# Memory attention of the decode rows: queries and probabilities as 32-column weights in four column groups

## The reference

```python
def _mem_attend(q, mk, mv):
    logits = jnp.einsum('bqhd,bshd->bhqs', q, mk.astype(q.dtype), preferred_element_type=jnp.float32) * (C_HD ** -0.5)
    p = jax.nn.softmax(logits, axis=-1)
    o = jnp.einsum('bhqs,bshd->bqhd', p.astype(q.dtype), mv.astype(q.dtype))
    return o.reshape(q.shape[0], q.shape[1], C_HEADS * C_HD)
...
    oc = _mem_attend(qc.reshape(Bsz, L, C_HEADS, C_HD), mem_k, mem_v)
```

## Time and profile before

| | us |
|---|---|
| median of 3 runs | 2118.42 |
| lowest, highest | 2112.59, 2127.39 |
| profiled execution, own time | 2127.54 |
| span of its profile | 2125.7 |
| mean granted clock of TensorE | 0.988 |
| decode stage in the profile, from the first gate product | 894.9 to 1078.9 |

### The profile page before, as it was taken

The page is one execution under the profiler, slowest core; times in us unless marked ns, Lnnn a source line. Parts: engine busy times, 40 slices in busy tenths (PEclk is TensorE's granted clock), DMA queues, the critical chain, the costliest instruction groups (busy, mean ns, idle before and its releaser), DMA issues.

```text
span 2125.7 us, 34336 instructions
## 1 busy us (share of the span) xinstructions
PE 2082.0 (98%) x13455; PEld 2011.8 (95%) x13455; DVE 999.6 (47%) x1765; ACT 524.6 (25%) x1143; POOL 737.0 (35%) x318
## 2 busy tenths in 40 slices
PE   6999999999999999999999999999999999999998
PEld 6999999999999999999889987999999999999997
DVE  5754720455555555411337945452534344343435
ACT  5333521344333344321032222200000000000002
POOL 3334763111111111121035432334444434444344
PEclk9999999999999999999799999999999999999999
DMA  6224333433222232263185431211111111111114
GB/s 194 79 80 111 105 97 110 128 101 102 73 64 85 83 102 66 60 172 118 60 273 192 161 138 62 72 41 49 39 49 39 49 47 46 45 49 39 49 40 174
DMA packets 221287, 193.79 MB, mean 91 GB/s; under 512 B 24731, under 2 KB 192283, under 8 KB 221170
## 3 DMA queue, kind: packets, MB, share of 16 engines
q1 hardware_dynamic: 207058, 182.72, 27.9%
q10 hardware_dynamic: 14128, 9.65, 1.4%
HBM read 146.26 MB, written 47.09 MB: 91 GB/s over the span
## 4 chain that ended last, share of the span: by engine, by line
PE 87%; DVE 6%; DMA 2%; issue 1%; ACT 1%; SPq 1%; POOL 0%; DVEq 0%; POOLq 0%; ACTq 0%
PE psum L1485 24%; PE psum L984 13%; PE psum L1546 11%; PE psum L1173 6%; PE psum L1101 6%; PE psum L1500 5%; PE psum L1251 4%; PE psum L1477 4%; PE psum L1220 2%; PE psum L1193 1%; PE psum L1209 1%; ACT pr L1817 1%; PE psum L1008 1%; PE psum L1049 1%; DVE asm L2282 1%
## 5 line engine op out<-in xcount | busy, mean ns | idle before, releaser
L842 POOL TENSOR_TENSOR wsp<-raw,kc 128x1024 fp32r<-128x1024 f32 x115 | 276.4, 2404 | 1151.8 <-PE psum L1173 423.5
L1485 PE MATMUL psum<-actD,wsp 128*128 128x352 f32 x3168 | 515.8, 323 | 1.0 <-ACT sg L2021 0.6
L1485 PEld LDWEIGHTS psum<-actD,wsp 128*128 128x128 f32 x3168 | 509.1, 188 | 1.5 <-issue 0.9
L845 POOL TENSOR_TENSOR wsp<-raw,wsp 128x1024 fp32r<-128x1024 f32 x115 | 281.8, 2451 | 9.0
L984 PE MATMUL psum<-actT,wsp 128*128 128x352 f32 x1656 | 272.7, 325 | 0.0
L984 PEld LDWEIGHTS psum<-actT,wsp 128*128 128x128 f32 x1656 | 267.9, 190 | 0.3
L2594 DVE TENSOR_TENSOR accT<-accT,psum 128x352 f32<-128x352 f32 x504 | 241.7, 520 | 50.1 <-PE psum L1546 50.1
L1546 PE MATMUL psum<-fT,wsp 128*128 128x352 f32 x1512 | 249.8, 323 | 0.4 <-DVE accT L2594 0.4
L1546 PEld LDWEIGHTS psum<-fT,wsp 128*128 128x128 f32 x1512 | 244.0, 188 | 0.7 <-DVE accT L2594 0.7
L1173 PE MATMUL psum<-actT,wsp 128*128 128x352 f32 x1152 | 216.5, 333 | 0.0
L2577 DVE TENSOR_TENSOR fr<-psum,sg 128x352 f32<-128x352 f32 x66 | 34.5, 524 | 375.4 <-PE psum L1485 373.1
(11 more groups left out here) (433 smaller groups left out, 2621.4 us busy)
## 6 DMA issues: line engine op xcount, KB each, us to landing
raw<-in_w_in SPq DMA_DIRECT2D x100, 256.0 KB, 4.0
raw<-in_w_ffn_in SPq DMA_DIRECT2D x88, 256.0 KB, 3.1
gat<-s_gate SPq DMA_DIRECT2D x12, 1056.0 KB, 5.1
raw<-in_w_ffn_out SPq DMA_DIRECT2D x44, 256.0 KB, 2.7
s_gate<-gst SPq DMA_DIRECT2D x48, 176.0 KB, 1.9
s_qkv<-y SPq DMA_DIRECT2D x12, 528.0 KB, 3.0
brw<-s_br SPq DMA_DIRECT2D x3, 2112.0 KB, 9.7
raw<-in_w_branch SPq DMA_DIRECT2D x24, 256.0 KB, 5.4
```

Of the source, the lines that this page charges most:

```text
L842: pool.tensor_tensor(wsp[:, slot, 0], raw[:, slot], ones.unsqueeze(1).to_broadcast([P, KT, P]), ALU.mult).then_inc(w_hi, 1)
L845: pool.tensor_tensor(wsp[:, slot, 1], raw[:, slot], wsp[:, slot, 0].bitcast(F32), ALU.subtract).then_inc(w_lo, 1)
L1485: mm = pe.matmul(psum[:, bank, 0:CH], wsp[:, slot, a, k, :], actD[:, h, k, CH * c:CH * c + CH], start=(k == 0 and q == 0), stop=(k == KT - ...
```

## The change

The scores turn the roles round: the queries become the weights and the transposed keys are streamed. `qw` holds for each head 8 blocks of 36 columns, zero but for the 4 query columns at the start of each. The 32 columns from 32 b on then hold the 4 queries of memory b in columns 4 b to 4 b + 3 and zeros elsewhere. The product for head h writes partitions 32 h to 32 h + 31 of bank 6 (one of four column groups), with all 256 keys streamed, and adds to what the other memories wrote there. So the rows of the softmax stand in bank 6 at once, and `mem_s`, the score transposes and the tile `mS` go. The values do the same with the probabilities: `pw`, one tile for each half of the memory, is filled by ACT from `mem_pt`, and the products stream 128 value columns of each head. Their sum has decode rows on partitions, so DVE copies it out (`mem_c`, tile `mC`) and one transpose (`mem_o`) follows. DVE fills `qw` and the second `pw` with zeros (`qw0`, `pw0`) and copies the queries (`qw`). The second `pw` shares `kvw` with the window keys, whose tile `wkv` is split for this.

The order changes too: the window scores alternate between rows 0 to 63 and 64 to 127 for each sequence, without the 14 gate products between; 20 gate products follow at once; `mem_values(6)` comes right behind `update(6)`, and `mem_values(7)` 14 gate products later and ahead of `update(7)`.

```diff
-    wkv = sb("wkv", [P, 2, DB, P], on=cE)
+    kvw = sb("kvw", [P, DB * P + 4 * DB * 36], on=cE)
+    kw_v, kw_k = (kvw[:, DB * P * x:DB * P * x + DB * P].rearrange("p (b d) -> p b d", b=DB) for x in range(2))
...
-    mS = sb("mS", [P, 2, P], on=cE)
...
-    pad = sb("pad", [P, 216], on=mid)
+    pad = sb("pad", [P, 344], on=mid)
...
+    mC = sb("mC", [P, P], on=mid)
+    qw = sb("qw", [P, 4, DB * 36], on=mid)
+    pw = (qw, kvw[:, DB * P:].rearrange("p (h x) -> p h x", h=4))
...
+    own_step = lambda ap: ap.rearrange("p h (b x) -> p h b x", x=36)[:, :, :, 0:DS]
...
             for h in range(4):
-                for t in range(2):
-                    mm = pe.matmul(psum[:, 5, P * t + DS * h + 16 * b:P * t + DS * h + 16 * b + DS], ckT[:, h, P * t:P * t + P],
-                                   da[:, 4 + h, DS * b:DS * b + DS], start=True, stop=True)
-            mm.then_inc(m_sc, 1)
+                mm = pe.matmul(psum[NS * h:NS * h + NS, 6, 0:MEM], qw[:, h, NS * b:NS * b + NS], ckT[:, h, :],
+                               start=(b == 0), stop=(b == DB - 1))
+            if b < DB - 1:
+                mm.then_inc(m_sc, 1)
+            else:
+                done(mm, "mem_rows")
...
-            for h in range(4):
-                for t in range(2):
-                    mm = pe.matmul(psum[:, 6, 2 * P + NS * h + DS * b:2 * P + NS * h + DS * b + DS], ck[:, b % 2, t, P * h:P * h + P],
-                                   mS[:, t, 16 * b + DS * h:16 * b + DS * h + DS], start=(t == 0), stop=(t == 1))
+            for t in range(2):
+                for h in range(4):
+                    mm = pe.matmul(psum[NS * h:NS * h + NS, 6, 2 * P:3 * P], pw[t][:, h, NS * b:NS * b + NS], ck[:, b % 2, t, P * h:P * h + P],
+                                   start=(b == 0 and t == 0), stop=(b == DB - 1 and t == 1))
...
-        for v in range(2):
-            rows = slice(64 * v, 64 * v + 64)
-            bank = (4, 7)[v]
-            for b in range(DB):
-                pe.matmul(psum[:, bank, 0:P].rearrange("p (g b s) -> p g b s", g=4, b=DB)[:, :, b, :], wkT[rows, b, :],
+        for b in range(DB):
+            for v, rows in enumerate((HA, HB)):
+                pe.matmul(psum[:, 4 + 3 * v, 0:P].rearrange("p (g b s) -> p g b s", g=4, b=DB)[:, :, b, :], wkT[rows, b, :],
                           da[rows, 0:4, DS * b:DS * b + DS], start=True, stop=True)
-            mm = pe.matmul(psum[0:Dn, bank, 256:256 + P], ext[rows, 0, :], da[rows, 0:4, :], start=True, stop=True)
-            if v == 0:
-                gate_mm(14)
+        for v, rows in enumerate((HA, HB)):
+            mm = pe.matmul(psum[0:Dn, 4 + 3 * v, 256:256 + P], ext[rows, 0, :], da[rows, 0:4, :], start=True, stop=True)
         done(mm, "new_sc")
-        gate_mm(6)
-        pe.wait_ge(f_ac, ACn("mem_s"))
-        for t in range(2):
-            mm = pe.transpose(psum[:, 6, P * t:P * t + P], mS[:, t, :], ident)
-        done(mm, "mem_rows")
-        gate_mm(14)
+        gate_mm(20)
...
         update(6)
-        gate_mm(6)
         mem_values(6)
+        gate_mm(14)
+        done(mem_values(7), "mem_v")
         gate_mm(10)
         update(7)
-        done(mem_values(7), "mem_o")
+        pe.wait_ge(f_dv, DVn("mem_c"))
+        done(pe.transpose(psum[:, 6, 3 * P:4 * P], mC[:], ident), "mem_o")
         gate_mm(576 - Gates.n)
...
-        act.wait_ge(m_sc, 1 + DB)
-        fdone(act.activation(flat(mS[:]), psum[:, 5, 0:256], ACT.Copy), "mem_s")
...
-        copy_e("mem_p", flat(mS[:]), psum[:, 6, 0:256], "mem_pt")
+        act.wait_ge(f_pe, PEn("mem_pt"))
+        act.wait_ge(f_dv, DVn("pw0"))
+        for t in range(2):
+            mm = act.activation(own_step(pw[t]), psum[:, 6, P * t:P * t + P].rearrange("p (h b s) -> p h b s", h=4, b=DB), ACT.Copy)
+        fdone(mm, "mem_p")
...
+        f("qw0", dve.memset(qw[:], 0.0))
+        own("qw0")
+        f("qw", dve.tensor_copy(own_step(qw), da[:, 4:8, :].rearrange("p h (b s) -> p h b s", b=DB)))
...
+        f("pw0", dve.memset(kvw[:, DB * P:], 0.0))
...
+            if j == 6:
+                dve.wait_ge(f_pe, PEn("mem_v"))
+                f("mem_c", dve.tensor_copy(mC[:], psum[:, 6, 2 * P:3 * P]))
...
-        f("mem_o", dve.tensor_copy(dob[:, 2], q4(6, 2, P)))
+        f("mem_o", dve.tensor_copy(dob[:, 2], q4(6, 3, P)))
```

More of the change, by code:

```diff
@@ L286, in build @@
     QI = (0, 1, 2, 3, 5, 6)
+    HA, HB = slice(0, 64), slice(64, 128)
     A_SC = [AHD ** -0.5] * 4 + [P ** -0.5] * 2
@@ L348, in build @@
     LOAD_G = {0: 18, 1: 19, 2: 20, 5: 21, 9: 22, 10: 23}
-    PE_E = ("out", "win_kt0", "bcast", "win_kt1", "x0", "new_sc", "mem_rows", "y", "win_rows", "xt", "mem_pt", "u_w",
-            "win_pt", "w_q_s", "vn", "win_o", "o", "sumsq", "mem_o")
-    AC_E = ("kv_out", "new_out", "tail_out", "wkT0", "dec", "rq", "wkT1", "mem_s", "x0", "win_s", "y", "mem_exp",
+    PE_E = ("out", "win_kt0", "bcast", "win_kt1", "mem_rows", "x0", "new_sc", "y", "win_rows", "xt", "mem_pt", "u_w",
+            "win_pt", "w_q_s", "vn", "win_o", "o", "sumsq", "mem_v", "mem_o")
+    AC_E = ("kv_out", "new_out", "tail_out", "wkT0", "dec", "rq", "wkT1", "x0", "win_s", "y", "mem_exp",
             "win_exp", "win_sk", "mem_p", "win_p", "vn", "sq", "root")
-    DV_E = ("ug", "d0", "d1", "d2", "d3", "mr", "kb", "kd", "vb", "dcm", "at0", "at", "kq", "x_", "xt0", "at1", "eg",
-            "el", "mem_mx", "mem_nm", "win_m0", "win_m1", "win_mx", "win_nx", "win_nm", "win_sk", "mem_rd", "mem_n",
+    DV_E = ("ug", "d0", "d1", "d2", "d3", "mr", "qw0", "qw", "kb", "kd", "vb", "dcm", "at0", "at", "kq", "x_", "xt0", "at1", "eg",
+            "el", "mem_mx", "mem_nm", "pw0", "win_m0", "win_m1", "win_mx", "win_nx", "win_nm", "win_sk", "mem_rd", "mem_n",
             "xt", "win_dn", "win_rd", "win_n", "uT", "wT", "vT", "qe", "vm0", "win_c0", "win_c1", "win_o0", "win_o1",
-            "o_", "s_e", "n0", "n1", "n2", "oq", "oz", "n3", "o_z", "vm1", "mem_o")
+            "o_", "s_e", "n0", "n1", "n2", "oq", "oz", "n3", "o_z", "vm1", "mem_c", "mem_o")
+    own_step = lambda ap: ap.rearrange("p h (b x) -> p h b x", x=36)[:, :, :, 0:DS]
     PEn, ACn, DVn = (lambda s: PE_E.index(s) + 1), (lambda s: AC_E.index(s) + 1), (lambda s: DV_E.index(s) + 1)
@@ L1274, in _ @@
         for b in range(4):
-            mm = pe.transpose(psum[:, 7, P * b:P * b + P], wkv[:, 0, b, :], ident)
+            mm = pe.transpose(psum[:, 7, P * b:P * b + P], kw_k[:, b, :], ident)
         done(mm, "win_kt0")
@@ L1296, in _ @@
         for b in range(4):
-            mm = pe.transpose(psum[:, 7, P * b:P * b + P], wkv[:, 0, 4 + b, :], ident)
+            mm = pe.transpose(psum[:, 7, P * b:P * b + P], kw_k[:, 4 + b, :], ident)
         done(mm, "win_kt1")
@@ L1423, in _ @@
         for b in range(DB):
-            pe.matmul(psum[:, 3, 0:256].rearrange("p (a b s) -> p a b s", a=8, b=DB)[:, :, b, :], wkv[:, 1, b, :],
+            pe.matmul(psum[:, 3, 0:256].rearrange("p (a b s) -> p a b s", a=8, b=DB)[:, :, b, :], kw_v[:, b, :],
                       sS[:, 0:2, :].rearrange("p v (g b s) -> p (v g) b s", g=4, b=DB)[:, :, b, :], start=True, stop=True)
@@ L1846, in _ @@
         for x in range(2):
-            act.dma_start(wkv[:, x], io[("state_win_k", "state_win_v")[x]].rearrange("b s v d -> s b (v d)")).then_inc(f_in, 16)
+            act.dma_start((kw_k, kw_v)[x], io[("state_win_k", "state_win_v")[x]].rearrange("b s v d -> s b (v d)")).then_inc(f_in, 16)
         act.dma_start(dmk[:], io["k_dmask"]).then_inc(f_in, 16)
```

## The result

The changed kernel takes 2092.47 us (median of 4 runs, 2090.66 to 2094.71) against 2117.52 us before (4 runs, 2112.59 to 2127.39): a ratio of 0.9884, 95% interval [0.9863, 0.9905], 25 us faster. The forecast was 2106 us with a range of 2097 to 2120. The direction was right and the gain was twice the forecast one, 25 us for 12. In the two profiled executions the spans are 2125.7 and 2092.9 us, 32.8 us apart.

What follows compares the result with a forecast made beforehand. It took PE's queue in the decode stage ahead of `update(7)` as the bound: the median 2118.4 us less 6.6 us of queue and 6.1 us of clock gave 2106 us, with 2097 to 2120 us for 8 in 10.

Steps and rivals of the forecast that it cites:

- What bounds it and where to look: Whole kernel: TensorE is busy for 98% of the span, so shortening its own queue in the decode stage counts.
- the stagger: Scores and values: one instruction's two passes can't overlap, neighbouring heads' can; five slots a score step, nine a memory's values.
- rival of fuller overlap: Scores and values: both passes of an instruction hidden too, 0.69 us for either; 2101 to 2096 us, chance 0.12.
- Drain: Scores and values: entering and leaving a group of 32-column products costs 0.24 us a visit.
- Window scores: Window scores on alternating row halves: loads may run two at once; -1.0 us, ends -1.8 and -0.2.
- The wait ahead of `mem_values(0)`: Ahead of the first memory's values: PE waits for `mem_p`, which sits behind `gates(13)`; 0.4 us, ends 0 and 1.
- DVE's fills: Zero fills of `qw` and the second `pw`: 0.97 us each, hidden in DVE's waits.
- The sum at the full clock: PE's queue ahead of `update(7)`: all terms together -6.6 us overlapped, +5.9 us in turn.
- The clock: Decode stage: wider streams leave one fall, at the window scores, of about 6.4 us costing 3.2; median gains 6.1 us.
- What the end hangs on: Behind the stage: a 31.3 us chain from the last state addition, so only what moves `update(7)` moves the end.

Runs made afterwards that it cites:

- e4: The kernel before with 96 instead of 4 columns streamed in each memory score and value product (results wrong): 2113.03 us, ratio 0.9973 to the kernel before.
- e1: The changed kernel with all four heads' score products written to one column group (scores wrong): 2105.5 us, one execution.
- e7: The changed kernel with `update(7)` right behind `update(6)`, ahead of the values of memories 6 and 7: 2092.59 us.
- e8: The changed kernel with `update(7)` right behind `update(6)` and the values of the memories moved earlier: 2085.58 us, ratio 0.9854 to the kernel before.
- e12: The changed kernel with scores in two column groups (scores wrong) and window scores in blocks of two, two and four sequences per row half: 2097.7 us, one execution.
- e2: The changed kernel with the two loops of the values exchanged, both memory halves for one head after the other: 2098.5 us, one execution.
- e3: The changed kernel with window scores for all sequences on rows 0 to 63, then all on rows 64 to 127: 2099.1 us, one execution.

## Why the prediction was wrong, step by step

- **What bounds it and where to look**: right. PE's queue in the decode stage was the place; the span before the stage is the same (key loop at 926.2 and 926.0 us).
- **The mis-sized step is the stagger.** I said that two passes of one instruction stand next to each other in the queue, so that a step's eight passes make five slots and a memory's sixteen make nine. They make two and four. That the two passes of one instruction can't overlap was right, but the next head doesn't wait for them. A score step costs 0.57 us and about 0.1 us on entry (17 gate products from 926.83 to 929.73, 2.90 us for 2.80) instead of 1.35; over eight -8.2 us instead of -2.8. A memory's values cost 0.68 us in the same way instead of 1.25; 8 x 0.68 - 12.0 = -6.5 us instead of -2.0. These two terms make 9.9 of the 10.5 us by which the sum was off. My rival of fuller overlap had this mechanism with 0.69 us for either, at 0.12, and held against it exactly the step that failed.
- **Drain**: 0.24 us a visit was about right. 8 passes in two waves take 2 x 0.2225 = 0.45 us, so 0.12 us of the 0.57 and the 0.1 on entry are the change of mode. The Trainium skill, TensorEngine Tiling (Array Packing), Key Properties, has both the drain and the tiles that run in parallel; this trace agrees with both.
- **Window scores**: about -1.6 us at the full clock for -1.0, near the better of my two ends. 32 passes in turn would be 3.4 us (0.107 each) to 3.6 us (0.112 each), 1.89 us was measured.
- **The wait ahead of `mem_values(0)`**: forecast 0.4 us, measured 0.44 us, released by ACT's `mem_p`. Its cause is the one given: `gates(13)` now ends behind.
- **DVE's fills**: 1.02 us each for 0.97, hidden. The wait for `bcast` fell from 11.67 to 10.20 us, and that for the window rows was 6.79 us long after the second fill.
- **The sum at the full clock.** -8.2 - 6.5 - 1.6 - 0.2 - 1.0 + 0.4 = -17.1 us instead of -6.6. The profiles agree: from the first key transposes to the last state addition it is 1076.51 - 926.22 = 150.3 us before and 1042.72 - 925.99 = 116.7 us after. Of these 33.6 us, 16.7 are the clock (half of 36.8 us less half of 3.4 us), which leaves 16.9 us.
- **The clock**: mechanism right, and e4 shows it: 4.2 us of the median, 2 to 9 by its interval, with one fall left, up to 1 us more of work and 2 us more of waits behind the stage. I took 6.1 us. I expected one fall around the window scores; there it was, 3.4 us long for the 6.4 that I took. But it is not in every execution: the profiles of e1, e7, e8 and e12, whose window scores also have no gate products between, have none there.
- **What the end hangs on**: wrong, and harmless by luck. I read the chain from the last state addition and concluded that only what moves `update(7)` counts. Most of PE's waits behind the stage, 4.2 of 5.3 us, hang on the load of `brw`, which SP had issued 8.6 us before that addition. The span fell by 32.8 us, and the end of `mem_values(5)` moved by (1062.42 - 926.22) - (1029.31 - 925.99) = 32.9 us, the last state addition by 33.6 us, so the forecast's sum, made up to `update(7)`, lost little by it. The chain of waits names the last of several things that SP waits for in order; what sets the pace for these waits is the loads behind `mem_values(5)`. e8 moves them, and the waits go; e7 moved the addition by 1.7 us and took away 0.5 us of waits.

What stays open: the median fell by 25.05 us. The parts with a measurement, 17.1 us of queue and, by e4, 4 to 7 us of clock, less 1.5 us of new waits behind the stage, make 20 to 23 us. The interval of e4 alone is wide enough for the rest. One more estimate points the same way: over the 31 runs of the kernel before in the three series, a run is about 1.4 us shorter for each 0.001 of mean granted clock, and the mean went from 0.990 to 0.9965 with the change, which would make the clock's part about 9 us. I didn't settle it.

## What to carry to other kernels

A product that streams a few columns past a 128-column weight pays for the weight load. With the roles changed and the heads put on different column groups the cost was that of the fullest group, and their order mattered little with up to four passes in a row on one group. The values that stream next to nothing also let the clock fall, and it costs all the work around them: padding the streamed side to 96 columns cost almost nothing (1.76 us for 1.70, e4). And before trusting the first link of the chain behind a stage, read what the DMA queue issued ahead of it, and check in the trace that an edit meant to move a link did: here the pace was mostly set by loads queued on SP behind another instruction, and DVE's order held back what e7 was to move.

## What the hardware showed that I had not expected

- Four f32 passes on four column groups start within 0.02 us, and the second passes of the same instructions 0.24 us later together, although first and second pass belong to one instruction. The Trainium skill, TensorE: Matmul & The Clock Gate, Part 3, has matmuls start in strict program order. e2 and e12 don't fit this: with two instructions of a head in a row, the last head's first pass still starts 0.044 us after the first one's, and not after the passes of the six instructions ahead of it.
- Between row halves the reach of this is four passes. A block of eight or sixteen passes on one half of the rows keeps the other half out until four are left to start (e3, e12).
- Two halves of the rows load their 128-column weights at the same time, as the paired starts in the trace show: 32 passes in 1.89 us, 0.059 us each, where one half alone takes 0.112 us a pass.
